# A two-layer transformer stack on one core: the feed-forwards' first products, with the rounded input and its rest side by side in one 512-column product

## The reference

```
def swiglu_2(h, w_in, w_out):
    gate, up = jnp.split(h @ w_in, [D_FF_2], axis=-1)
    return (jax.nn.silu(gate) * up) @ w_out
...
        x = x + swiglu_2(rmsnorm_2(x, norm_ffn[l]), ffn_w_in[l], ffn_w_out[l])
```

## Time and profile before

| | |
|---|---|
| median of 3 runs | 1152.67 us (1152.48 to 1154.0) |
| the profiled execution | 1154.97 us, of which 1153.7 us are the span |
| granted TensorE clock over the span | 0.996 of full speed |
| PE busy | 1129.4 us, 98% of the span |
| DVE busy | 661.6 us, 57% |
| ACT busy | 575.5 us, 50% |
| POOL busy | 293.8 us, 25% |

### The profile page before, as it was taken

One profiled execution on the slowest core, in us unless ns is written; L12 is line 12 of the kernel. 1 busy time (PEld: TensorE's weight loads), 2 busy tenths in 40 slices (PEclk: granted clock), 3 DMA queues, 4 the chain that ended last, 5 costly groups with the idle time before them and its releaser, 6 DMA issues.

```text
span 1153.7 us, 19296 instructions
## 1 busy us (share of the span) xinstructions
PE 1129.4 (98%) x8117; PEld 1047.5 (91%) x8117; DVE 661.6 (57%) x1034; ACT 575.5 (50%) x881; POOL 293.8 (25%) x193
## 2 busy tenths in 40 slices
PE   7999999999999999999999999999999979999997
PEld 6999989999989999889988889999889969999986
DVE  6655765677656454338897656343248776543424
ACT  6646555555545644337623444444435935444432
POOL 2022100000005444512411115444410002544440
PEclk9999999999999999999999999999999989999999
DMA  8679474644547666655543348665545344766550
GB/s 261 228 224 328 142 240 130 188 149 144 184 146 221 180 187 198 201 164 173 178 146 110 118 154 291 193 189 188 201 155 193 110 144 130 217 186 187 189 189 36
DMA packets 155152, 207.48 MB, mean 180 GB/s; under 512 B 9471, under 2 KB 128409, under 8 KB 155066
## 3 DMA queue, kind: packets, MB, share of 16 engines
q1 hardware_dynamic: 151274, 193.11, 52.8%
q0 software_dynamic: 3792, 13.15, 3.4%
HBM read 205.01 MB, written 4.24 MB: 181 GB/s over the span
## 4 chain that ended last, share of the span: by engine, by line
PE 89%; DVE 6%; ACT 3%; DMA 1%; issue 1%; POOL 0%; SPq 0%; DVEq 0%; ACTq 0%; POOLq 0%
PE bank L491 18%; PE bank L494 18%; PE bank L497 18%; PE bank L514 9%; PE bank L508 9%; PE bank L511 9%; PE bank L847 2%; DVE wlo L1341 2%; PE bank L773 1%; PE bank L783 1%; DMA area<-in_hgrn_lb 1%; PE bank L795 1%; PE bank L554 1%; ACT whi L944 1%; DVE uc L1471 0%
## 5 line engine op out<-in xcount | busy, mean ns | idle before, releaser
L1341 DVE TENSOR_TENSOR wlo<-raw,whi 128x1024 fp32r<-128x1024 f32 x275 | 338.8, 1260 | 226.1 <-ACT whi L944 225.1
L944 ACT ACTIVATE whi<-raw 128x1024 fp32r<-128x1024 f32 x362 | 360.3, 1044 | 107.4 <-PE bank L514 102.8
L1904 POOL TENSOR_TENSOR wlo<-raw,whi 128x1024 fp32r<-128x1024 f32 x87 | 223.2, 2565 | 256.0 <-ACT whi L944 256.0
L491 PE MATMUL bank<-hh,whi 128*128 128x256 f32 x1784 | 286.3, 282 | 1.7 <-ACT hh L976 1.7
L494 PE MATMUL bank<-hh,wlo 128*128 128x256 f32 x1784 | 281.8, 279 | 0.0
L497 PE MATMUL bank<-hl,whi 128*128 128x256 f32 x1784 | 281.5, 279 | 0.0
L491 PEld LDWEIGHTS bank<-hh,whi 128*128 128x128 f32 x1784 | 241.8, 188 | 6.7 <-issue 5.5
L494 PEld LDWEIGHTS bank<-hh,wlo 128*128 128x128 f32 x1784 | 240.8, 188 | 0.0
L497 PEld LDWEIGHTS bank<-hl,whi 128*128 128x128 f32 x1784 | 240.7, 188 | 0.0
L1911 POOL TENSOR_TENSOR st<-st,half 128x1 f32<-128x1 f32 x18 | 10.3, 580 | 345.6 <-DVE st L1358 317.5
L508 PE MATMUL bank<-whi,gh 128*128 128x512 f32 x264 | 81.5, 390 | 0.0
(11 more groups left out here) (308 smaller groups left out, 1228.2 us busy)
## 6 DMA issues: line engine op xcount, KB each, us to landing
raw<-in_ffn_w_in SPq DMA_DIRECT2D x88, 512.0 KB, 3.8
raw<-in_w_in SPq DMA_DIRECT2D x72, 512.0 KB, 5.0
raw<-in_ffn_w_out SPq DMA_DIRECT2D x44, 512.0 KB, 3.3
raw<-in_hgrn_w_in SPq DMA_DIRECT2D x32, 512.0 KB, 4.4
raw<-in_w_ffn_gate SPq DMA_DIRECT2D x22, 512.0 KB, 4.5
raw<-in_w_ffn_up SPq DMA_DIRECT2D x22, 512.0 KB, 4.5
raw<-in_w_ffn_down SPq DMA_DIRECT2D x22, 512.0 KB, 3.5
raw<-in_w_branch SPq DMA_DIRECT2D x16, 512.0 KB, 4.4
```

The costliest lines, as they stand in the source:

```text
L491: T.matmul(out, wh[:, i, c], xh[:, k, :], start=first and (i, k) == pairs[0], stop=False)
L944: A.activation(half_of(whi, j, h), half_of(raw, j, h), ACT.Copy).then_inc(s_hi[j % NS][h], 1)
L1341: V.tensor_tensor(half_of(wlo, j, h), half_of(raw, j, h), half_of(whi, j, h).bitcast(f32), ALU.subtract).then_inc(s_lo[j % NS][h], 1)
L1904: G.tensor_tensor(half_of(wlo, j, 1), half_of(raw, j, 1), half_of(whi, j, 1).bitcast(f32), ALU.subtract).then_inc(s_lo[j % NS][1], 1)
```

## The change

For the feed-forwards (`WIDE` names their inputs 2, 5 and 7) the input now lies in one tile `ex` of 8 blocks x 512 columns: the rounded input in columns 0 to 255, its rest in 256 to 511. `eh` and `el` become views of it. One product of `whi` with all 512 columns takes the place of the two of 256; the product of `wlo` goes on having 256 columns and is added to the left half. An output of 128 columns so fills a whole bank, a unit two banks, and the units rotate over the pairs (0,1), (2,3), (4,5), (6,7). VectorE adds left and right half by a `tensor_reduce` over both banks (`summed`), into `sg` for the gate and a new tile `ug` for up; the multiplications that read the bank before now read SBUF. `apart` keeps one group of `project_pair` in the old form.

```
         shifted = ExitStack()
-        eh = sbuf(shifted, "eh", [128, 8, 256], f32r)
-        el = sbuf(shifted, "el", [128, 8, 256], f32r)
+        ex = sbuf(shifted, "ex", [128, 8, 512], f32r)
         shifted.close()
...
         sbuf(root, "gap_stage", [128, 72])
-        banks = [root.enter_context(nc.psum_tensor(f"bank{i}", [128, 512], f32)) for i in range(8)]
+        psum = root.enter_context(nc.psum_tensor("bank", [128, 8, 512], f32))
+        banks = [psum[:, i, :] for i in range(8)]
...
             ffn.append((sbuf(ctx, f"gh_{f}", [128, 22, 256], f32r), sbuf(ctx, f"gl_{f}", [128, 22, 256], f32r),
-                        sbuf(ctx, f"sg_{f}", [128, 2, 512]), sbuf(ctx, f"bc_f{f}", [128, 256])))
+                        sbuf(ctx, f"sg_{f}", [128, 2, 512]), sbuf(ctx, f"bc_f{f}", [128, 256]), sbuf(ctx, f"ug_{f}", [128, 512])))
             ctx.close()
...
         lr.close()
+        eh, el = ex[:, :, 0:256], ex[:, :, 256:512]
...
+        WIDE = (2, 5, 7)
+        def parts_of(e):
+            return (eh, el) if e in WIDE else (hh, hl)
         def hh_set(e, k):
...
+            def joint(b, j, m, ks, e, i0=0, first=True, last=True, apart=False):
+                wh, wl = whole(whi, j), whole(wlo, j)
+                c = slice(128 * m, 128 * m + 128)
+                n = units[j][1] // 2
+                pairs = list(enumerate(ks, i0))
+                for h in range(2):
+                    of_half = [(i, k) for i, k in pairs if i // n == h]
+                    for i, k in of_half:
+                        tq.wait_ge(*hi_set(j, h))
+                        tq.wait_ge(*hh_set(e, k))
+                        if apart:
+                            T.matmul(banks[b][:, 0:256], wh[:, i, c], eh[:, k, :], start=first and (i, k) == pairs[0], stop=False)
+                        else:
+                            tq.wait_ge(*hl_set(e, k))
+                            t = T.matmul(banks[b][:, :], wh[:, i, c], ex[:, k, :], start=first and (i, k) == pairs[0], stop=False)
+                    for i, k in of_half:
+                        tq.wait_ge(*lo_set(j, h))
+                        t = T.matmul(banks[b][:, 0:256], wl[:, i, c], eh[:, k, :], start=False, stop=last and not apart and (i, k) == pairs[-1])
+                    if apart:
+                        for i, k in of_half:
+                            tq.wait_ge(*hl_set(e, k))
+                            t = T.matmul(banks[b][:, 256:512], wh[:, i, c], el[:, k, :], start=False, stop=last and (i, k) == pairs[-1])
+                return t
+            def project_joint(key, e):
+                j = unit_at[key]
+                b = turn(("col", *key, 0), next_bank(), 0)
+                turn(("col", *key, 1), b + 1)
+                for m in range(2):
+                    tq.wait_ge(*free(("col", *key, m)))
+                    t = joint(b + m, j, m, range(8), e)
+                t.then_inc(s_full[b + 1], 1)
+                used[j, 0] = used[j, 1] = full("col", *key, 1)
             def moving(out, j, t, xh, xl, ks, c0, n, hi, lo, first=True, last=True):
...
                 js = [unit_at[key] for key in keys]
-                bs = [turn(("col", *key), next_bank(), 2) for key in keys]
+                if e in WIDE:
+                    bs = [turn(("col", *key, 0), next_bank(), 0) for key in keys]
+                    ends = [turn(("col", *key, 1), b + 1, 2) for key, b in zip(keys, bs)]
+                else:
+                    bs = ends = [turn(("col", *key), next_bank(), 2) for key in keys]
                 for part in range(2):
...
                         for m in range(2):
+                            if e in WIDE:
+                                if part == 0:
+                                    tq.wait_ge(*free(("col", *keys[i], m)))
+                                tok = joint(bs[i] + m, j, m, range(4 * part, 4 * part + 4), e, i0=4 * part, first=part == 0,
+                                            last=part == 1, apart=part == 1 and i == m == 0)
+                                continue
                             if part == 0:
...
                                         *of_norm(e), i0=4 * part, first=part == m == 0, last=part == m == 1)
-                        tok.then_inc(s_full[bs[i]], 1)
-                        used[j, part] = (s_full[bs[i]], turns["col", *keys[i]][2] - 1 + part)
+                        tok.then_inc(s_full[ends[i]], 1)
+                        used[j, part] = (s_full[ends[i]], fills_of[ends[i]] - 1 + part)
                         if part == 1 and i == 0:
...
-            rot_banks[0] = [0, 1, 2, 3]
-
             def feed_forward(f, e, e2):
+                rotation[0], rot_banks[0] = 0, [0, 2, 4, 6]
                 project_pair([("g", f, 0), ("u", f, 0)], e)
                 for j in range(1, 11):
-                    project_columns(("g", f, j), e)
-                    project_columns(("u", f, j), e)
+                    project_joint(("g", f, j), e)
+                    project_joint(("u", f, j), e)
+                rot_banks[0] = [0, 1, 2, 3]
                 gh, gl = ffn[f][0:2]
...
                     aq.wait_ge(*full("tr", e, q))
-                    A.activation(hh[:, 2 * q:2 * q + 2, :], two(bank_of("tr", e, q)[:, :]), ACT.Copy).then_inc(s_hh, 1)
+                    A.activation(parts_of(e)[0][:, 2 * q:2 * q + 2, :], two(bank_of("tr", e, q)[:, :]), ACT.Copy).then_inc(s_hh, 1)
...
             def feed_forward(f, e, e2, again=None):
-                gh, gl, sg, bc = ffn[f]
+                gh, gl, sg, bc, ug = ffn[f]
                 def gate_of(j):
-                    aq.wait_ge(*evac("col", "g", f, j))
+                    aq.wait_ge(*evac("col", "g", f, j, 1))
                     A.activation(sg[:, j % 2, :], sg[:, j % 2, :], ACT.Silu).then_inc(s_silu, 1)
...
                 def up_of(j):
-                    aq.wait_ge(*evac("col", "u", f, j))
+                    aq.wait_ge(*evac("col", "u", f, j, 1))
                     A.activation(gh[:, 2 * j:2 * j + 2, :], two(sg[:, j % 2, :]), ACT.Copy).then_inc(s_gh, 1)
...
                     vq.wait_ge(*hh_set(e, 2 * q))
-                    V.tensor_tensor(hl[:, sl, :], two(bank_of("tr", e, q)[:, :]), hh[:, sl, :].bitcast(f32),
+                    xh, xl = parts_of(e)
+                    V.tensor_tensor(xl[:, sl, :], two(bank_of("tr", e, q)[:, :]), xh[:, sl, :].bitcast(f32),
                                     ALU.subtract).then_inc(evacuated("tr", e, q), 1)
...
             def feed_forward(f, e, e2, again=None):
-                gh, gl, sg, bc = ffn[f]
+                gh, gl, sg, bc, ug = ffn[f]
+                def summed(dst, *key):
+                    b = turns["col", *key, 0][0]
+                    vq.wait_ge(*full("col", *key, 1))
+                    V.tensor_reduce(out=dst, in_=psum[:, b:b + 2, :].rearrange("p m (s t) -> p m t s", s=2), op=ALU.add,
+                                    axis=mybir.AxisListType.X).then_inc(evacuated("col", *key, 0), 1)
+                    vq.wait_ge(*evac("col", *key, 0))
...
                         vq.wait_ge(s_gl, 11 * f + j - 1)
-                    scaled(two(sg[:, j % 2, :]), ("g", f, j), e, bc)
+                    s = two(sg[:, j % 2, :])
+                    summed(s, "g", f, j)
+                    vq.wait_ge(*evac("fac", e))
+                    V.tensor_tensor(s, s, bc[:, :].rearrange("p (o t) -> p o t", o=1).broadcast_to([128, 2, 256]),
+                                    ALU.mult).then_inc(evacuated("col", "g", f, j, 1), 1)
...
                     s = sg[:, j % 2, :]
+                    summed(two(ug[:, :]), "u", f, j)
                     vq.wait_ge(s_silu, 11 * f + j + 1)
-                    vq.wait_ge(*full("col", "u", f, j))
-                    V.tensor_tensor(s, s, bank_of("col", "u", f, j)[:, :], ALU.mult).then_inc(evacuated("col", "u", f, j), 1)
+                    V.tensor_tensor(s, s, ug[:, :], ALU.mult).then_inc(evacuated("col", "u", f, j, 1), 1)
                     vq.wait_ge(s_gh, 11 * f + j + 1)
```

## The result

The changed kernel takes 1167.63 us (median of 4 runs, 1166.33 to 1168.63), the kernel before on the same chip 1152.76 (4 runs): ratio 1.0121, 95% interval 1.0108 to 1.0135. It is 1.2% slower, where 1143.5 us and "faster" had been forecast, with a range of 1138.5 to 1150.6. The profiled execution took 1168.63 us.

What follows compares the result with a forecast made beforehand. TensorE was taken to bound the kernel: 1044 steps at 8.8 ns save 9.2 us, 1154.97 to 1145.8; less 2.3 for the median of the runs gives 1143.5 us, range 1138.5 to 1150.6.

Steps and rivals of the forecast that it cites:

- What bounds the kernel: Feed-forward first products: TensorE busy 100 of 100 us at full clock, so the end moves by what its stream gets shorter.
- the number of steps: Three feed-forwards: 1056 steps of one block for one half unit, less 4 kept apart in each, leaving 1044.
- the sum's form: Whole kernel: only TensorE's saving of 9.2 us counts; VectorE's added work and later hand-overs are zero in the sum.
- The price of a wide product: First products: 226.7 ns for 512 columns, so a step takes 344.4 instead of 353.2 ns, 8.8 less.
- rival B: First products: the wide product costs 233.5 ns, the gain is 2.1 us, the time 1150.6 us; chance 0.20.
- At least 2.6 us are left, so I put all of it at nothing: Evacuation ahead of `whi` and `wlo`: slack 5.7 us, less about 1.3 for reduction and hand-over, up to 1.8 for blocking.
- a blocked multiplication: VectorE multiplication with both inputs in SBUF beside GpSimd: 0.69 to 2.48 us, up to 1.8 us more than before.
- My check of VectorE: First products, per pair of units: VectorE's work grows from 5.2 to 8.1 us and fits in TensorE's 11.0.
- C: Rival: VectorE's reduction, reading pairs 256 columns apart in a bank, takes much longer; at 3.3 us, 1182 us; chance 0.05.
- D: Rival: GpSimd blocks VectorE so often that part of the gain goes, needing 2.9 us a pair; about 1150 us; chance 0.05.
- Start of a feed-forward: First wide products want the rest at once; it is ready in time, so this costs nothing.
- last pair: Its evacuation grows by about 1.3 us, but its `gh` is used eight down units later, so zero.

Runs made afterwards that it cites:

- run 1: Changed kernel, but the reduction writes its sum to PSUM bank 7, so multiplications read a bank; units rotate over three pairs of banks: 1153.92 us, ratio 0.9999.
- run 2: Changed kernel with three pairs of banks and no reductions: multiplications read the left halves, a one-column copy frees the banks: 1154.34 us, ratio 1.0003.
- run 5: Two small Exp operations with table loads added on ScalarE in the second feed-forward: on the changed kernel 1171.27 us (1.0147), with the sum in bank 7 1153.74 (0.9997).

## Why the prediction was wrong

**What bounds the kernel, the number of steps, the sum's form:** right. In runs 1 and 2 the stages take 115.51 us with the reduction and without it: what TensorE's products cost, once nothing else holds them.

**The price of a wide product: the first step that failed.** I took 226.7 + 117.7 = 344.4 ns, "what the stages right behind it show with tiles that have no 64-byte shift, as `ex` has none". It is 351.1, so a step gives 2.1 ns instead of 8.8 (2.5 by the stages), and 1044 of them 2.2 us (2.6) instead of 9.2. That is rival B's price, whose low bound of 2.0 was in the text. Two rates of the same kernel for 512 columns, 226.7 and 233.5, stood there, and I chose by one property of the address. But in both of these rows the tile is the stationary operand, and in the changed kernel `ex` is the streamed one. For a stationary tile the choice was right: `hh` and `ex` cost 233 ns with the shift and 227 without. It says nothing of a streamed tile: `ex` without a shift costs 232.5, with one 230.6, and at none of the five places 226.7. With its loop open, the change is worth nothing that can be measured (0.9999). The Trainium skill (TensorE: Matmul & The Clock Gate, Back-to-back issue gap) gives its rule for an isolated product; by it a step would save 2.5 ns, an estimate, and the trace's 2.1 to 2.5 ns agree, though its absolute prices are too low here, as the prediction said.

**"At least 2.6 us are left, so I put all of it at nothing": the step that turned the sign.** Both parts had been sized correctly: the reduction was put at 1.22 us and measured 1.22, and a blocked multiplication was put at "up to 1.8 more" and measured 0.95 more (1.64). The error was to set them against the slack of one evacuation, once. Slack that is used again every unit must be compared as a rate: the round from one `whi` to the next, against TensorE's time for a unit. The rows were there: `whi` 1.99 and GpSimd's `wlo` 2.49, and with 0.08 between them, 0.55 from GpSimd's end to that of a held multiplication and 0.57 up to the next `whi` they make 5.68. The 0.55 and 0.57 needed a look at how a held operation ends, which the earlier trace rows showed for one of 1024 elements (it ended 1.08 us behind GpSimd's), and at what is queued behind it. My check of VectorE, 8.1 of 11.0 us in a pair, "it fits", added up work (measured 77.7 us in 100, 8.7 of 11.2) and was true; a loop over three engines at 44 to 78% each can still be full.

**Why only the first feed-forward stalls in its first products.** The deficit of the loop, 0.06 us a unit, needs some 20 units to show; in the second and third feed-forward it comes out at the start of the second products, as waits for GpSimd's `wlo` and 2.1 us each. In the first, six rounds come on top that are longer than 5.69 us. Two have a table load (7.21 us each). Three (6.32, 6.24 and 6.09) come behind VectorE's small `hn` and `vec` operations, which make its `wlo` late, and GpSimd's beside it takes 2.90 to 3.13 us instead of 2.49. The longest is 7.96 us: at 434.16, behind seven such operations, VectorE's own `wlo` is held by GpSimd's, which has just begun. Together they are 7.0 us over 5.68 each. That the small operations are a cause is read from these rows; run 5 tested only the table loads.

```profile
434.16 3.40 DVE L1395 TENSOR_TENSOR wlo<-raw,whi 128x1024 fp32r<-128x1024 f32 x1
...
437.61 0.74 PE L527 MATMUL bank<-ex,wlo 128*128 128x256 f32 x4 [2.17 <-DVE wlo L1395]
```

The waits that the trace lists in that stage come to 4.1 us, since it counts a wait only from the modelled end of the product before. From start to start, against 232.5 and 118.5 ns a product, the late starts come to 6.2 us. Behind the longest of them the granted clock is 0.51 from 438.20 to 441.60, the 1.2 GHz level: the four wide, four narrow and four wide products from 438.19 to 442.06 take 3.87 us instead of 2.34, another 1.5. Together that is 7.7 us, all of the 6.9 that the stage is longer and the 0.8 that its products are cheaper.

**The rivals.** C named the reduction and was wrong: two banks read in pairs 256 columns apart cost 1.22 us, as much as 1024 elements side by side. D named the right engine, GpSimd holding VectorE, but asked for 2.9 us a pair because it compared with VectorE's capacity; 1.9 us a pair were enough, as they lay in the loop. Start of a feed-forward and last pair: nothing seen there beyond 0.3 us, as put. No wait of TensorE for a bank is listed either.

**What stays open.** What in an address makes a product cheap or dear: five places of `ex` give 113.9 to 116.3 us a stage without a rule that I could state. And run 1 should have gained 2.5 us by its stages, while its interval ends at 1.3 us gained. In its profile the span is 1.0 us shorter: 0.9 of the 2.5 are lost in the start-up part, and 0.6 between the second and third feed-forward, where the granted clock is at 0.5, the 1.2 GHz level, for 10.2 us instead of 6.8. Whether the change causes either, one profile of each kernel can't tell.

## What to carry to other kernels

Where an engine's program is in order, follow the slack around the loop, not along one evacuation: if the delayed operation is what releases the next round of the work that delays it, only the round's length against the bound engine's period counts, and every extra delay stays. A test is to look whether the helper still waits for the bound engine; as long as it does, there is slack. Put one input of a VectorE operation that runs beside GpSimd into PSUM, when a bank is free, before giving work to another engine. And a saving of 2% in matmul prices is not to be counted on until the new tile has been timed at its address and in its role, stationary or streamed.

## What the runs showed of the hardware

A VectorE multiplication of 512 elements with two SBUF inputs that begins beside a GpSimd `wlo` ended 0.54 to 0.56 us after it, in all 56 cases of the changed kernel: mostly 1.64 us instead of 0.69. A subtraction of 1024 elements ended 1.08 or 1.09 us after it (16 cases). With one input in a bank a multiplication was not held at all (0.69 us in all 59 cases of run 1). The Trainium skill (SBUF — State Buffer, section SBUF: two separate sides) describes this as an exclusive lock that is held for the whole instruction; the traces agree, and cutting GpSimd's instruction in two did not help, since VectorE arrived behind the first piece. Unexpected was the effect of the tile's address on TensorE: 64 bytes changed narrow products from 117.7 to 120 ns with `hh` streamed, a step from 351 to 346 ns with `ex` streamed, and a 512-column product from 227 to 233 ns with `hh` or `ex` stationary. A strided `TENSOR_REDUCE` over two banks, 1024 elements to 512, took 1.22 us.
